# One stage for the rotation and the values' projection of a latent attention

## The chip, the cores and the metric

The kernel runs on one core of a Trainium2 chip. Its time is the device time of one execution in microseconds; the kernel before takes 3262.89 us, the median of three runs (3262.27 to 3264.33). The reader needs five of the core's engines: TensorE (PE, with its weight loads PEld), VectorE (DVE), ScalarE (ACT), GpSimd (POOL), and SyncE (SP), which issues DMA transfers here. Each works through its own list of instructions in order and waits on semaphores.

## The reference, cut to what matters

The program is two transformer blocks. The change lies in the second mixer of the first block, an attention over 256 context and 512 latent tokens whose keys and values come from a latent of 256 numbers per token:

```
def mla_q(q_a, q_norm, w_uq, rope):
    q = (rmsnorm(q_a, q_norm) @ w_uq).reshape(B, L, MLA_HEADS, MLA_NOPE + MLA_ROPE)
    q_n, q_r = jnp.split(q, [MLA_NOPE], axis=-1)
    return jnp.concatenate([q_n, apply_rope2d(q_r, *rope)], axis=-1)

def mla_kv(kv_a, k_r, kv_norm, w_ukv, rope):
    kv = (rmsnorm(kv_a, kv_norm) @ w_ukv).reshape(B, L, MLA_HEADS, MLA_NOPE + MLA_V)
    k_n, v = jnp.split(kv, [MLA_NOPE], axis=-1)
    if rope is not None:
        k_r = apply_rope2d(k_r, *rope)
    ...
```

Two things in it matter here. The rotated parts (64 numbers per head of the queries, 64 shared ones of the keys) go through `apply_rope2d`. The values v of all 8 heads are one product: 768 tokens by 256, times 256 by 1024.

## The kernel before, in words

The kernel is a sequence of stages. Each stage is one block: all engines start it together, after a barrier, and the next one starts when all have left it. Semaphores come from two sets that take turns; the GpSimd clears those of the stage before.

Every matrix product is made of three passes. An operand x is kept as two rounded parts, x.high (a copy on ACT in the type float32r) and x.low (on DVE, x minus x.high), and `three_passes` (L304 to L306) adds high*high, high*low and low*high into one bank of PSUM, the accumulator memory, which has 8 banks of 512 numbers per partition.

The attention's preparation is six stages in a row (function `mla`); the last three are those of the change:

1. `rotate_split` rotates five tiles of 128x512: four of queries, one of keys. Per tile: PE multiplies it with a permutation into one of banks 0 to 3 (L2336), DVE multiplies by the cosine (L2356), multiplies the bank by the sine (L2358) and adds both (L2359), ACT makes the high part (L2344), DVE the low part (L2352). A sixth piece, the context's keys, is only split (L2341 and L2352).
2. `project_tokens` for the first 512 columns of the values. SP loads 512 KB of weights (L1576), ACT and DVE split them in two steps (L1595, L1605), PE meanwhile runs eight products whose result nobody reads (`keep_running`, L290), then makes six sums, one for each 128 tokens, of six matmuls each. ACT copies a finished sum to v.high (L1599), DVE writes v.low (L1616), which frees the bank. Four banks are used in turn.
3. The same for the other 512 columns, over the same places for the weights.

After them the stage of the attention itself starts, whose first instruction on PE is a score's matmul (L304).

The queries and keys before rotation, the cosine, the sine and a scratch tile lie where v is written. The weights' place held the queries' latent, which nothing reads any more once these three stages begin. What is read of the latent of keys and values lies behind it.

Of the kernel before, what the change touches and what calls it, by code (L numbers as in the profile page):

```python
# [28 lines left out]
ALU = mybir.AluOpType  # L29
AX = mybir.AxisListType  # L30

P = 128
D = 1024
DT = D // P
CTX = 256
# [64 lines left out]
H_LOW_AT = DT * T  # L100
# [1463 lines left out]
def project_tokens(k, weights, dst, kt, x, token_tiles, width, col=None, at=None):  # L1564

    nc = k.nc
    k.stage()
    at = MEM - 3 * kt * width if at is None else at
    raw = k.plain(at, kt, width)
    w = Pair(k, at + kt * width, at + 2 * kt * width, kt, width)  # L1570
    landed, rounded, ready, product, cut, taken = (k.sem(s) for s in ("landed", "rounded", "ready", "product", "cut", "taken"))
    n_tiles = len(token_tiles)
    with k.block() as block:
        @block.sync
        def _(sp):
# [25 lines left out]
        @block.vector  # L1601
        def _(dve):
            for kk in range(kt):
                dve.wait_ge(rounded, kk + 1)
                nc.vector.tensor_tensor(w.low[:, kk, :], raw[:, kk, :], w.high_plain[:, kk, :],  # L1605
                                        ALU.subtract).then_inc(ready, 1)
            for j in range(n_tiles):
                if col is None:
                    dve.wait_ge(product, j + 1)
                    bank = k.bank(j % 4, width)  # L1610
                    parts = dst[:, j].shape
                    nc.vector.tensor_copy(dst[:, j], bank.rearrange("p (h n) -> p h n", n=parts[2]) if len(parts) == 3 else bank
                                          ).then_inc(taken, 1)
# [708 lines left out]
            in_turns(dve, turns, turn)  # L2322


def rotate_split(k, parts, cos, sin, scratch, plain=()):

    nc = k.nc
    k.stage()
    partner, summed, rounded = k.sem("partner"), k.sem("summed"), k.sem("rounded")
    with k.block() as block:  # L2330
        @block.tensor
        def _(pe):
            for n, (x, *out) in enumerate(parts):
                if n >= 4:
                    pe.wait_ge(summed, n - 3)
                nc.tensor.matmul(k.bank(n % 4), k.const("rot_gqa"), x, start=True, stop=True).then_inc(partner, 1)  # L2336

        @block.scalar
        def _(act):
            for x, high, high_plain, low in plain:  # L2340
                nc.scalar.copy(high, x).then_inc(rounded, 1)  # L2341
            for n, (x, high, high_plain, low) in enumerate(parts):
                act.wait_ge(summed, n + 1)
                nc.scalar.copy(high, x).then_inc(rounded, 1)  # L2344

        @block.vector
        def _(dve):
            chain = Chain(dve, k.sem("chain"))

            def cut(n, x, high, high_plain, low):  # L2350
                dve.wait_ge(rounded, n + 1)
                nc.vector.tensor_tensor(low, x, high_plain, ALU.subtract)  # L2352

            todo = list(plain) + list(parts)
            for n, (x, *out) in enumerate(parts):
                chain.link(nc.vector.tensor_tensor(scratch, x, cos, ALU.mult))  # L2356
                dve.wait_ge(partner, n + 1)
                chain.link(nc.vector.tensor_tensor(x, k.bank(n % 4), sin, ALU.mult))  # L2358
                nc.vector.tensor_tensor(x, x, scratch, ALU.add).then_inc(summed, 1)  # L2359
                dve.wait_ge(summed, n + 1)  # L2360
                for m in range(len(plain) if n == 0 else 0):
                    cut(m, *todo[m])
                if n:
                    cut(len(plain) + n - 1, *parts[n - 1])
            cut(len(todo) - 1, *parts[-1])


def load(k, pairs):
# [11 lines left out]
def mla(k, norm):  # L2380
    low = k.plain(MLA_V_AT, 6, T)
    qr_plain = k.plain(MLA_V_AT + 6 * T, 4, LAT)
    at = MLA_V_AT + 6 * T + 4 * LAT
    cos, sin, scratch = (k.words(at + j * LAT, at + (j + 1) * LAT) for j in range(3))
    qa = Pair(k, H_LOW_AT, H_LOW_AT + 3 * LAT, 3, LAT, CTX)
    kva = Pair(k, H_LOW_AT + 6 * LAT, H_LOW_AT + 6 * LAT + 2 * T, 2, T)
    kn = Pair(k, H_HIGH_AT, WORK_AT, 8, T)
    at = WORK_AT + 8 * T
    qn, at = Pair(k, at, at + 8 * LAT, 8, LAT, CTX), at + 16 * LAT
    qr, at = Pair(k, at, at + 4 * LAT, 4, LAT, CTX), at + 8 * LAT  # L2390
    kr = Pair(k, at, at + T, 1, T)
# [10 lines left out]
    rotate_split(k, [(qr_plain[:, n, :], qr.high[:, n, :], qr.high_plain[:, n, :], qr.low[:, n, :]) for n in range(4)]  # L2402
                 + [(low[:, 5, CTX:T], kr.high[:, 0, CTX:T], kr.high_plain[:, 0, CTX:T], kr.low[:, 0, CTX:T])],
                 cos, sin, scratch, [(low[:, 5, 0:CTX], kr.high[:, 0, 0:CTX], kr.high_plain[:, 0, 0:CTX], kr.low[:, 0, 0:CTX])])
# [1316 lines left out]
```

## Time and profile before

| | |
|---|---|
| median of three runs | 3262.89 us |
| the profiled execution's own time | 3258.2 us |
| its span, first to last instruction | 3256.1 us |
| TensorE busy | 2944.3 us, 90% |
| VectorE busy | 1692.2 us, 52% |
| ScalarE busy | 1211.8 us, 37% |
| mean granted TensorE clock | 0.948 of full |

The profile is of one execution. Times inside it are microseconds from the span's first instruction. The granted clock is the share of full speed that TensorE was given: 1.00 is 2.4 GHz, 0.50 is 1.2 GHz. In an interval's row "PEq" is PE's own instruction sequencer, so idle time that ended with it ended by a barrier or a branch and not by data. The three stages of the change run from 1493.6 to 1540.4 us.

### The profile page before, as it was taken

To read this page: it belongs to the slowest core of one execution; us is meant where nothing else is said; L and a number is where in the kernel's file an instruction comes from. 1 tells how busy PE (TensorE), PEld (TensorE's weight loads), DVE (VectorE), ACT (ScalarE), POOL (GpSimd) and SP (SyncE) were. 2 spreads that over 40 slices of the span, in tenths; PEclk is the share of its full clock that TensorE was granted. 3 is DMA by queue.
4 is the path that set the end of the run, shared out by engine and by line. 5 is a ranking of instruction groups with operands and counts; after the bars stand their busy time and mean duration, and the time that the engine had idled before them with its cause. 6 is when DMAs were issued, how large, how long until landed. Compare 5 with 4: busy or idle time off the path is not lost. (4 is left out here: it accounts for less than half of the span.)

```text
span 3256.1 us, 37947 instructions
## 1 busy us (share of the span) xinstructions
PE 2944.3 (90%) x14226; PEld 2338.0 (72%) x14226; DVE 1692.2 (52%) x2385; ACT 1211.8 (37%) x1621; POOL 167.1 (5%) x127
## 2 busy tenths in 40 slices
PE   7899988799999899897999999989878888899996
PEld 3674776687888888675777887867755567777775
DVE  5444323634767443434654343352366553788886
ACT  2320231424232232423433433244424323477774
POOL 0000001100011000000000000000000100122220
PEclk9899998899999999999999999999979799999998
DMA  8300110021345142110002221212200013699996
GB/s 356 127 27 13 52 52 2 27 90 52 123 147 175 59 149 97 52 36 26 1 27 89 92 103 64 95 60 84 77 8 1 1 52 125 252 366 355 361 339 243
DMA packets 76008, 362.78 MB, mean 111 GB/s; under 512 B 13170, under 2 KB 17043, under 8 KB 50292
## 3 DMA queue, kind: packets, MB, share of 16 engines
q1 hardware_dynamic: 62356, 327.66, 27.9%
q0 software_dynamic: 13536, 33.58, 3.0%
q8 instruction: 72, 1.18, 0.1%
q14 instruction: 44, 0.36, 0.0%
HBM read 360.67 MB, written 16.25 MB: 116 GB/s over the span
## 5 line engine op out<-in xcount | busy, mean ns | idle before, releaser
L304 PE MATMUL ps<-rounded,rounded 128*128 128x512 f32 (+3 forms) x3700 | 1377.0, 372 | 139.9 <-DVE rounded L2237 24.2
L305 PE MATMUL ps<-rounded,rounded 128*128 128x512 f32 (+3 forms) x3700 | 1337.6, 362 | 0.0
L306 PE MATMUL ps<-rounded,rounded 128*128 128x512 f32 (+3 forms) x3700 | 1336.0, 361 | 0.0
L304 PEld LDWEIGHTS ps<-rounded,rounded 128*128 128x128 f32 (+1 forms) x3700 | 706.6, 191 | 322.6 <-issue 113.8
L306 PEld LDWEIGHTS ps<-rounded,rounded 128*128 128x128 f32 (+1 forms) x3700 | 707.0, 191 | 107.2
L305 PEld LDWEIGHTS ps<-rounded,rounded 128*128 128x128 f32 (+1 forms) x3700 | 708.5, 191 | 94.8
L283 DVE TENSOR_TENSOR rounded<-work,rounded 128x1024 fp32r<-128x1024 f32 (+3 forms) x224 | 306.6, 1371 | 840.7 <-ACT rounded L279 840.4
L279 ACT CAST rounded<-work 128x1024 fp32r<-128x1024 f32 (+3 forms) x224 | 261.6, 1169 | 740.2 <-PE ps L306 617.2
L3472 DVE TENSOR_TENSOR rounded<-work,rounded 128x2048 fp32r<-128x2048 f32 x138 | 309.8, 2287 | 71.9 <-ACT rounded L3300 71.9
L3300 ACT CAST rounded<-work 128x2048 fp32r<-128x2048 f32 x138 | 259.5, 1915 | 78.0 <-PE ps L306 78.0
L290 PE MATMUL ps<-cst 128*128 128x256 f32 x530 | 143.7, 432 | 64.7 <-PEq L170 64.7
L290 PEld LDWEIGHTS ps<-cst 128*128 128x128 f32 x530 | 113.8, 220 | 90.3 <-issue 72.5
L279 ACT ACT_TABLE_LOAD x34 | 43.6, 1283 | 207.1 <-PE ps L306 198.4
L478 DVE SCALAR_TENSOR_TENSOR work<-work,silu_c 128x256 f32<-128x256 f32 x224 | 103.7, 484 | 13.1 <-DMA work<-in_ada_w 7.3
L2756 POOL TENSOR_TENSOR h<-work,row 128x2048 f32<-128x2048 f32 x2 | 9.2, 4637 | 1486.8 <-DVE row L2838 1486.8
L1017 DVE SCALAR_TENSOR_TENSOR work<-ps,vec,work 128x255 f32 (+4 forms) x116 | 72.5, 654 | 20.4 <-ACT work L987 14.4
L1095 ACT ACTIVATE work<-work 128x768 f32<-128x768 f32 (+1 forms) x44 | 32.6, 740 | 126.7 <-DVE work L1130 126.7
L2237 DVE TENSOR_TENSOR rounded<-ps,rounded 128x768 fp32r<-128x768 f32 (+1 forms) x64 | 52.3, 817 | 40.3 <-ACT rounded L2204 40.3
L1386 PE MATMUL ps<-work 128*128 128x512 f32 x160 | 71.1, 603 | 0.0
L3184 POOL DMA_INDIRECT y_rows<-h,whole x23 | 51.5, 2240 | 345.6 <-ACT h L3338 345.6
L787 PE MATMUL ps<-work,silu_c 128*2 128x512 f32 x128 | 58.5, 612 | 10.8 <-DMA work<-in_ada_w 10.8
L2231 DVE TENSOR_REDUCE row<-ps 128x1 f32<-128x768 f32 (+1 forms) x64 | 52.5, 820 | 18.0 <-PE ps L306 17.8
(487 smaller groups left out, 2486.8 us busy)
## 6 DMA issues: line engine op xcount, KB each, us to landing
work<-in_moe SPq DMA_DIRECT2D x138, 1024.0 KB, 7.4
work<-in_ffn_up SPq DMA_DIRECT2D x44, 1024.0 KB, 4.8
work<-in_ffn_down SPq DMA_DIRECT2D x66, 512.0 KB, 3.4
work<-in_ada_w SPq DMA_DIRECT2D x12, 2048.0 KB, 18.0
work<-in_ada_w POOLq DMA_DIRECT2D x48, 512.0 KB, 4.0
work<-in_w_out SPq DMA_DIRECT2D x16, 512.0 KB, 3.6
work<-in_w_gates SPq DMA_DIRECT2D x16, 512.0 KB, 3.5
work<-in_w_in_hy SPq DMA_DIRECT2D x12, 512.0 KB, 3.4
```

Source lines behind the costliest of these rows:

```text
L279: self.k.nc.scalar.copy(self.parts[s][0], self.raw[s]).then_inc(self.rounded[s], 1)
L283: self.k.nc.vector.tensor_tensor(self.parts[s][1], self.raw[s], self.high_plain[s], ALU.subtract).then_inc(self.ready[s], 1)
L290: k.nc.tensor.matmul(k.bank(bank, 2 * P), k.const("ident"), k.cst[:, 0:2 * P], start=True, stop=True)
L304: k.nc.tensor.matmul(out, sh, mh, start=start, stop=False)
L305: k.nc.tensor.matmul(out, sh, ml, start=False, stop=False)
L306: return k.nc.tensor.matmul(out, sl, mh, start=False, stop=stop)
L478: done = self.k.nc.vector.scalar_tensor_tensor(out=total, in0=tile, scalar=by, in1=total, op0=ALU.mult, op1=ALU.add)
L787: last = nc.tensor.matmul(k.bank(n % 2)[0:2, :], k.silu_c[:, kk, :], wide[n % 3][:, kk * 512:(kk + 1) * 512], start=kk == 0, stop=kk == DT ...
L1017: nc.vector.scalar_tensor_tensor(out=out, in0=k.pair(p)[:, lo + o:hi + o], scalar=k.col(conv_w, n + tiles * (o + taps // 2)), in1=out, op0 ...
L1386: last = nc.tensor.matmul(bank(group, part), tab[part][:, a, n * P:(n + 1) * P], src[:, a, :], start=a == 0, stop=a == count - 1)
L3300: nc.scalar.copy(ring.parts[:, c % ring.SPLIT, 0, :], ring.raw[c % ring.RAW]).then_inc(ring.rounded, 1)
L3472: V.tensor_tensor(ring.parts[:, s, 1, :], ring.raw[c % ring.RAW], ring.plain[:, s, 0, :], ALU.subtract).then_inc(ring.ready, 1)
```

## The change

`rotate_split` and the two calls of `project_tokens` become one stage, `rotate_and_values`. The rotation keeps banks 0 to 3, the twelve sums of the values use banks 4 to 7 in turn. Both transfers of weights are issued in this stage, the second one once the first weights are split. The splitting of the first weights stands on ACT after the second query tile, on DVE after the third turn. PE makes the first four sums as soon as it has the weights. Because v lies over the rotation's inputs, ACT waits for DVE's last low part (semaphore `left`) before it copies the first sum. The weights of the second half are split after all six sums of the first half are made. The eight idle products of both `project_tokens` are gone. `k.stage()` is called once in place of three times.

```
-def rotate_split(k, parts, cos, sin, scratch, plain=()):
+def rotate_and_values(k, parts, cos, sin, scratch, plain, names, v, x, at):
...
+    width, kt, n_tiles = 512, 2, 6
+    raw, w = k.plain(at, kt, width), Pair(k, at + kt * width, at + 2 * kt * width, kt, width)
...
+    tiles = [(half, j) for half in range(2) for j in range(n_tiles)]
+
+    def sums(m):
+        return k.bank(4 + m % 4, width)
...
+        @block.sync
+        def _(sp):
+            for half, name in enumerate(names):
+                if half:
+                    sp.wait_ge(w_ready, kt)
+                sp.dma_start(raw, k.dram[name].rearrange("p (k n) -> p k n", n=width)).then_inc(landed, 16)
+
         @block.tensor
...
+            for m, (half, j) in enumerate(tiles):
+                if m >= 4:
+                    pe.wait_ge(taken, m - 3)
+                for kk in range(kt):
+                    if j == 0:
+                        pe.wait_ge(w_ready, kt * half + kk + 1)
+                    last = three_passes(k, sums(m), x.tokens(kk, j * P, (j + 1) * P), w.tokens(kk, 0, width), kk == 0, kk == kt - 1)
+                last.then_inc(product, 1)
 
         @block.scalar
         def _(act):
+            def weights(half):
+                act.wait_ge(landed, 16 * half + 16)
+                for kk in range(kt):
+                    nc.scalar.copy(w.high[:, kk, :], raw[:, kk, :]).then_inc(w_high, 1)
...
+                if n == 1:
+                    weights(0)
+            act.wait_ge(left, 1)
+            for m, (half, j) in enumerate(tiles):
+                if m == n_tiles - 1:
+                    act.wait_ge(product, n_tiles)
+                    weights(1)
+                act.wait_ge(product, m + 1)
+                nc.scalar.copy(v.high[:, j, half * width:(half + 1) * width], sums(m)).then_inc(cut, 1)
 
         @block.vector
...
+                if n == 2:
+                    weights(0)
+            split_off(len(todo) - 1, *parts[-1]).then_inc(left, 1)
+            for m, (half, j) in enumerate(tiles):
+                if m == n_tiles - 1:
+                    weights(1)
+                dve.wait_ge(cut, m + 1)
+                columns = slice(half * width, (half + 1) * width)
+                nc.vector.tensor_tensor(v.low[:, j, columns], sums(m), v.high_plain[:, j, columns], ALU.subtract).then_inc(taken, 1)
...
-    for half in range(2):
-        project_tokens(k, f"mla_w_v{half}", v, 2, kva, range(6), 512, half * 512, H_LOW_AT)
```

The order of ACT's instructions before, from the start of the rotation to the end of the values. `rounded_34816` and `rounded_37632` are the high parts of queries and keys, `rounded_8192` of the weights, `rounded_44544` of v; L170, L1591 and L2338 are the ends and starts of stages.

```order
L2338 UNCONDITIONAL_BRANCH
L2341 CAST rounded_37632_6878<-work 128x256
L2344 CAST rounded_34816_6876<-work 128x512 x4
L2344 CAST rounded_37632_6878<-work 128x512
L170 UNCONDITIONAL_BRANCH
L1591 UNCONDITIONAL_BRANCH
L1595 CAST rounded_8192_8190<-h 128x512 x2
L1599 CAST rounded_44544_6880<-ps 128x512 x6
```

The same place on ACT now:

```order
L2371 CAST rounded_37632_6878<-work 128x256
L2374 CAST rounded_34816_6876<-work 128x512 x2
L2368 CAST rounded_8192_8090<-h 128x512 x2
L2374 CAST rounded_34816_6876<-work 128x512 x2
L2374 CAST rounded_37632_6878<-work 128x512
L2383 CAST rounded_44544_6880<-ps 128x512 x5
L2368 CAST rounded_8192_8090<-h 128x512 x2
L2383 CAST rounded_44544_6880<-ps 128x512 x7
```

The first weights' copies have moved ahead of the third query tile's, the second weights' ahead of the sixth sum's.

On DVE before, from the low part in the fourth turn of the rotation to the end of the first half of the values (`rounded_36864` and `rounded_38400` are low parts of queries and keys, `rounded_9216` of the weights, `rounded_50688` of v):

```order
L2352 TENSOR_TENSOR rounded_36864_6877<-work,rounded_34816_6876 128x512
L2356 TENSOR_TENSOR work<-work 128x512
L2358 TENSOR_TENSOR work<-ps,work 128x512
L2359 TENSOR_TENSOR work<-work 128x512
L2352 TENSOR_TENSOR rounded_36864_6877<-work,rounded_34816_6876 128x512
L2352 TENSOR_TENSOR rounded_38400_6879<-work,rounded_37632_6878 128x512
L170 UNCONDITIONAL_BRANCH
L1601 UNCONDITIONAL_BRANCH
L1605 TENSOR_TENSOR rounded_9216_8191<-h,rounded_8192_8190 128x512 x2
L1616 TENSOR_TENSOR rounded_50688_6881<-ps,rounded_44544_6880 128x512 x6
```

Now on DVE, from the low part in the third turn on. One row of two more subtractions of weights and one of the seven last low parts of v follow, then the stage ends:

```order
L2391 TENSOR_TENSOR rounded_36864_6877<-work,rounded_34816_6876 128x512
L2396 TENSOR_TENSOR rounded_9216_8091<-h,rounded_8192_8090 128x512 x2
L2400 TENSOR_TENSOR work<-work 128x512
L2402 TENSOR_TENSOR work<-ps,work 128x512
L2403 TENSOR_TENSOR work<-work 128x512
L2391 TENSOR_TENSOR rounded_36864_6877<-work,rounded_34816_6876 128x512
L2400 TENSOR_TENSOR work<-work 128x512
L2402 TENSOR_TENSOR work<-ps,work 128x512
L2403 TENSOR_TENSOR work<-work 128x512
L2391 TENSOR_TENSOR rounded_36864_6877<-work,rounded_34816_6876 128x512
L2391 TENSOR_TENSOR rounded_38400_6879<-work,rounded_37632_6878 128x512
L2417 TENSOR_TENSOR rounded_50688_6881<-ps,rounded_44544_6880 128x512 x5
```

The first weights' two subtractions stand between the third and fourth turn of the rotation, and nothing stands any more between the rotation's last low part and the first of v.

## Rows read from the trace of the kernel before

**Rows 1.** The head of the page.
```profile
span 3256.1 us, 37947 instructions
```

**Rows 2.** Busy time in four stretches: the three stages, most of the attention.
```profile
core 0: us, PE busy (x) PEld busy (x) DVE busy (x) ACT busy (x) POOL busy (x), PEclk, DMA share, GB/s
1493.60:1508.50 14.90, 4.53 (x10) 1.82 (x10) 13.86 (x21) 3.51 (x6) 0.00 (x0) 0.80 0.00 0
1508.70:1524.00 15.30, 13.79 (x52) 11.10 (x52) 5.45 (x8) 4.67 (x8) 0.00 (x0) 0.87 0.11 34
1524.10:1540.50 16.40, 12.16 (x52) 9.64 (x52) 5.45 (x8) 4.68 (x8) 0.00 (x0) 1.00 0.11 33
1550.00:1680.00 130.00, 129.27 (x756) 98.32 (x755) 86.47 (x155) 50.79 (x97) 0.00 (x0) 1.00 0.00 1
```

**Rows 3.** Waits from 1493 to 1541: us in total, times, longest.
```profile
ACT rounded L1595 <- DMA h<-in_mla_w_v: 10.5, 2, 5.9
```

**Rows 4.** Order of time, rotation: start, us, engine, line, what, xcount [idle before <-releaser].
```profile
1493.62 0.41 ACT L2341 CAST rounded<-work 128x256 fp32r<-128x256 f32 x1 [1.28 <-PEq L170]
1493.64 4.53 PE L2336 MATMUL ps<-work,cst 128*128 128x512 f32 x10 [2.15 <-PEq L170]
...
1498.81 0.62 ACT L2344 CAST rounded<-work 128x512 fp32r<-128x512 f32 x1 [1.89 <-DVE work L2359]
...
1501.59 0.69 DVE L2352 TENSOR_TENSOR rounded<-work,rounded 128x512 fp32r<-128x512 f32 x1
1502.20 0.68 DVE L2356 TENSOR_TENSOR work<-work 128x512 f32<-128x512 f32 x1
...
1504.37 0.69 DVE L2352 TENSOR_TENSOR rounded<-work,rounded 128x512 fp32r<-128x512 f32 x1
...
1507.15 1.34 DVE L2352 TENSOR_TENSOR rounded<-work,rounded 128x512 fp32r<-128x512 f32 x2
```

**Rows 5.** Order of time, first half of the values.
```profile
1508.75 0.34 SPq L1576 DMA_DIRECT2D h<-in_mla_w_v  x1
1508.80 5.58 PE L290 MATMUL ps<-cst 128*128 128x256 f32 x16 [10.63 <-PEq L170]
1512.34 1.14 ACT L1595 CAST rounded<-h 128x512 fp32r<-128x512 f32 x2 [4.57 <-DMA h<-in_mla_w_v]
...
1523.24 0.69 DVE L1616 TENSOR_TENSOR rounded<-ps,rounded 128x512 fp32r<-128x512 f32 x1 [0.66 <-ACT rounded L1599]
```

**Rows 6.** Order of time, second half of the values, and the attention's first matmul.
```profile
1524.20 0.34 SPq L1576 DMA_DIRECT2D h<-in_mla_w_v  x1
...
1529.15 1.14 ACT L1595 CAST rounded<-h 128x512 fp32r<-128x512 f32 x2 [5.94 <-DMA h<-in_mla_w_v]
...
1530.55 0.50 PE L304 MATMUL ps<-rounded,rounded 128*128 128x512 f32 x1 [2.60 <-DVE rounded L1605]
...
1532.24 0.59 ACT L1599 CAST rounded<-ps 128x512 fp32r<-128x512 f32 x1 [1.95 <-PE ps L306]
...
1533.61 0.59 ACT L1599 CAST rounded<-ps 128x512 fp32r<-128x512 f32 x1 [0.78 <-PE ps L306]
...
1539.67 0.69 DVE L1616 TENSOR_TENSOR rounded<-ps,rounded 128x512 fp32r<-128x512 f32 x1 [0.67 <-ACT rounded L1599]
1540.68 0.35 PE L304 MATMUL ps<-rounded,rounded 128*128 128x256 f32 x1 [1.67 <-PEq L170]
```

**Rows 7.** Busy time and granted clock in four stretches.
```profile
485.30:488.60 3.30, 3.05 (x7) 2.47 (x8) 3.30 (x7) 3.12 (x6) 0.00 (x0) 0.50 0.00 0
1502.40:1505.80 3.40, 0.00 (x0) 0.00 (x0) 3.26 (x6) 0.62 (x1) 0.00 (x0) 0.50 0.00 0
1690.20:1693.50 3.30, 2.81 (x13) 2.81 (x14) 0.77 (x2) 0.00 (x0) 0.00 (x0) 0.50 0.00 0
2557.20:2598.00 40.80, 36.66 (x100) 21.02 (x101) 18.63 (x16) 11.82 (x40) 8.01 (x2) 0.50 0.00 1
```

**Rows 8.** Order of time: PE after idle time, elsewhere in the program.
```profile
485.55 0.79 PE L304 MATMUL ps<-rounded,rounded 128*128 128x512 f32 x1 [5.83 <-DVE rounded L1605]
...
486.57 0.63 PE L306 MATMUL ps<-rounded,rounded 128*128 128x512 f32 x1
487.00 0.63 PE L304 MATMUL ps<-rounded,rounded 128*128 128x512 f32 x1
...
1690.69 0.58 PE L304 MATMUL ps<-rounded,rounded 128*128 128x256 f32 x1 [1.88 <-DVE rounded L2237]
```

More of the change, by code:

```diff
@@ L2322, in _ @@
             in_turns(dve, turns, turn)
-def rotate_split(k, parts, cos, sin, scratch, plain=()):
+def rotate_and_values(k, parts, cos, sin, scratch, plain, names, v, x, at):
     nc = k.nc
     k.stage()
-    partner, summed, rounded = k.sem("partner"), k.sem("summed"), k.sem("rounded")
-    with k.block() as block:
+    width, kt, n_tiles = 512, 2, 6
+    raw, w = k.plain(at, kt, width), Pair(k, at + kt * width, at + 2 * kt * width, kt, width)
+    partner, summed, rounded, left = (k.sem(s) for s in ("partner", "summed", "rounded", "left"))
+    landed, w_high, w_ready, product, cut, taken = (k.sem(s) for s in ("landed", "w_high", "w_ready", "product", "cut", "taken"))
+    tiles = [(half, j) for half in range(2) for j in range(n_tiles)]
+    def sums(m):
+        return k.bank(4 + m % 4, width)
+    with k.block() as block:
+        @block.sync
[4 more added lines that the diff above has]
+                sp.dma_start(raw, k.dram[name].rearrange("p (k n) -> p k n", n=width)).then_inc(landed, 16)
@@ L2331, in _ @@
         @block.tensor
         def _(pe):
-            for n, (x, *out) in enumerate(parts):
+            for n, (y, *out) in enumerate(parts):
                 if n >= 4:
                     pe.wait_ge(summed, n - 3)
-                nc.tensor.matmul(k.bank(n % 4), k.const("rot_gqa"), x, start=True, stop=True).then_inc(partner, 1)
+                nc.tensor.matmul(k.bank(n % 4), k.const("rot_gqa"), y, start=True, stop=True).then_inc(partner, 1)
+            for m, (half, j) in enumerate(tiles):
[6 more added lines that the diff above has]
+                last.then_inc(product, 1)
@@ L2338, in _ @@
         @block.scalar
         def _(act):
-            for x, high, high_plain, low in plain:
-                nc.scalar.copy(high, x).then_inc(rounded, 1)
-            for n, (x, high, high_plain, low) in enumerate(parts):
-                act.wait_ge(summed, n + 1)
-                nc.scalar.copy(high, x).then_inc(rounded, 1)
+            def weights(half):
+                act.wait_ge(landed, 16 * half + 16)
+                for kk in range(kt):
+                    nc.scalar.copy(w.high[:, kk, :], raw[:, kk, :]).then_inc(w_high, 1)
@@ new lines, in _ @@
+            for y, high, high_plain, low in plain:
+                nc.scalar.copy(high, y).then_inc(rounded, 1)
+            for n, (y, high, high_plain, low) in enumerate(parts):
+                act.wait_ge(summed, n + 1)
+                nc.scalar.copy(high, y).then_inc(rounded, 1)
+                if n == 1:
[7 more added lines that the diff above has]
+                nc.scalar.copy(v.high[:, j, half * width:(half + 1) * width], sums(m)).then_inc(cut, 1)
@@ L2348, in _, with split_off, weights @@
             chain = Chain(dve, k.sem("chain"))
-            def cut(n, x, high, high_plain, low):
+            def split_off(n, y, high, high_plain, low):
                 dve.wait_ge(rounded, n + 1)
-                nc.vector.tensor_tensor(low, x, high_plain, ALU.subtract)
+                return nc.vector.tensor_tensor(low, y, high_plain, ALU.subtract)
+            def weights(half):
+                for kk in range(kt):
+                    dve.wait_ge(w_high, kt * half + kk + 1)
+                    nc.vector.tensor_tensor(w.low[:, kk, :], raw[:, kk, :], w.high_plain[:, kk, :], ALU.subtract).then_inc(w_ready, 1)
             todo = list(plain) + list(parts)
-            for n, (x, *out) in enumerate(parts):
-                chain.link(nc.vector.tensor_tensor(scratch, x, cos, ALU.mult))
+            for n, (y, *out) in enumerate(parts):
+                chain.link(nc.vector.tensor_tensor(scratch, y, cos, ALU.mult))
                 dve.wait_ge(partner, n + 1)
-                chain.link(nc.vector.tensor_tensor(x, k.bank(n % 4), sin, ALU.mult))
-                nc.vector.tensor_tensor(x, x, scratch, ALU.add).then_inc(summed, 1)
+                chain.link(nc.vector.tensor_tensor(y, k.bank(n % 4), sin, ALU.mult))
+                nc.vector.tensor_tensor(y, y, scratch, ALU.add).then_inc(summed, 1)
                 dve.wait_ge(summed, n + 1)
                 for m in range(len(plain) if n == 0 else 0):
-                    cut(m, *todo[m])
+                    split_off(m, *todo[m])
                 if n:
-                    cut(len(plain) + n - 1, *parts[n - 1])
-            cut(len(todo) - 1, *parts[-1])
+                    split_off(len(plain) + n - 1, *parts[n - 1])
+                if n == 2:
[7 more added lines that the diff above has]
+                nc.vector.tensor_tensor(v.low[:, j, columns], sums(m), v.high_plain[:, j, columns], ALU.subtract).then_inc(taken, 1)
 def load(k, pairs):
@@ L2401, in mla @@
     project_split(k, "mla_w_kn", kn, SEGS, 2, kva)
-    rotate_split(k, [(qr_plain[:, n, :], qr.high[:, n, :], qr.high_plain[:, n, :], qr.low[:, n, :]) for n in range(4)]
+    rotate_and_values(k, [(qr_plain[:, n, :], qr.high[:, n, :], qr.high_plain[:, n, :], qr.low[:, n, :]) for n in range(4)]
                  + [(low[:, 5, CTX:T], kr.high[:, 0, CTX:T], kr.high_plain[:, 0, CTX:T], kr.low[:, 0, CTX:T])],
-                 cos, sin, scratch, [(low[:, 5, 0:CTX], kr.high[:, 0, 0:CTX], kr.high_plain[:, 0, 0:CTX], kr.low[:, 0, 0:CTX])])
-    for half in range(2):
-        project_tokens(k, f"mla_w_v{half}", v, 2, kva, range(6), 512, half * 512, H_LOW_AT)
+                 cos, sin, scratch, [(low[:, 5, 0:CTX], kr.high[:, 0, 0:CTX], kr.high_plain[:, 0, 0:CTX], kr.low[:, 0, 0:CTX])],
+                      ("mla_w_v0", "mla_w_v1"), v, kva, H_LOW_AT)
     def rope_half(h):
```

## The prediction

> **What bounds the kernel now.** I read the head of the page first, for the span of 3256.1 us [rows 1], then the busy time by stretches, then who waits for whom, then the order of time. In the stretches the reader is to see that the three stages differ from the attention behind them. The attention has TensorE busy for 129.27 of 130 us; there only PE's work counts. The rotation has PE busy for 4.53 of 14.90 us and DVE for 13.86: it is bound by DVE. The two halves of the values hold the same 52 matmul records each, 16 of them idle products, and DVE is busy for 5.45 us in either [rows 2]. So PE is idle for most of the first stage, and DVE for most of the other two. In the waits the reader sees a second loss: ACT waits 10.5 us for the two transfers of weights [rows 3], since each is issued only when its own stage opens.
>
> In the order of time the rotation starts at 1493.6 and PE's ten records (five matmuls) are over at 1493.64 + 4.53 = 1498.17, while DVE ends at 1507.15 + 1.34 = 1508.49 [rows 4]. The first half then takes to 1523.24 + 0.69 = 1523.93 [rows 5], the second to 1540.36, and the attention's first matmul starts at 1540.68 [rows 6]. All that the change touches lies between 1493.6 and 1540.68. From the end of the rotation to the end of v are 1540.36 - 1508.49 = 31.87 us, and this is what I rebuild.
>
> **The first weights, under the rotation.** SP issues the transfer at about 1493.6. From issue to ACT's first copy the two transfers of before took 1512.34 - 1508.75 = 3.59 us [rows 5] and 1529.15 - 1524.20 = 4.95 us [rows 6]. ACT comes to the weights after its second query tile, at 1498.81 + 0.62 = 1499.43 [rows 4], 5.8 us after the issue: it finds them. Its two copies take 1.14 us [rows 6], to 1500.57. ACT's next tile is summed no sooner than 1501.59, where DVE goes on in step with it [rows 4], so ACT loses nothing. DVE reaches its two subtractions at 1502.20 and they stand in its list ahead of the fourth turn: a real cost, as DVE bounds the rotation. Two such subtractions are 1.34 us [rows 4]. If the transfer came later than about 7.5 us after its issue, each further microsecond would be one on DVE; I cost it at nothing, with the longer of the two transfers 2.5 us short of that.
>
> So the rotation ends at 1508.49 + 1.34 = 1509.83. **PE** has its first weights after one subtraction, at 1502.20 + 0.67, about 1502.9, and starts on four sums, 24 matmuls. In the steady pace of before a sum takes 1533.61 - 1532.24 = 1.37 us, 0.228 a matmul [rows 6], so the four would take 5.5 us.
>
> **The clock.** PE has then been idle from 1498.17 to 1502.9, 4.7 us. Nothing keeps it busy, since the idle products are gone. In the same stretch before, the granted clock had fallen to 0.50 by 1502.40 [rows 7], and a values' projection elsewhere, which also started after idle time (5.83 us), began at 0.50, with matmuls 487.00 - 486.57 = 0.43 us apart in place of 0.228 [rows 7, 8]. So I take the fall as certain. That one lasted from its first matmul at 485.55 to about 488.6, 3.1 us. At 0.43 all 24 matmuls take 10.3 us (to 1513.2); with 3 us at the low clock they take about 7 (to 1510). The bounds of this item at the point where the sums are needed: ACT copies the first at 1509.83 and, DVE behind it taking 0.69 a sum, the fourth is wanted from about 1511.7. With a low clock of up to 6 us the fourth is made by 1511.5 and the cost is zero; with one that lasts throughout, 1.5 us on this part alone. I take zero, the nearest row being the 3.1 us one. The Trainium skill, page "TensorE: Matmul & The Clock Gate", section "Why this matters for your kernels", warns against letting PE idle between bursts of matmuls, since the clock then falls back to half rate. By this rule alone, dropping the idle products speaks against the change. Taken to its end, with no recovery before the attention, it gives the time of the second rival below (3259.6); the sum here gives 3248.0. The row agrees that the clock falls; what the rule does not weigh is that these four sums wait for the rotation anyway.
>
> **From the rotation's end.** ACT was held by `left`; queued behind that wait are all of v's copies, and behind these DVE's low parts and, for its fifth sum on, PE. First copy 0.59, its low part 0.69 [rows 6], and 0.1 for the hand-overs between engines (an estimate: DVE idles 0.67 before a low part, 0.08 more than ACT's copy takes [rows 6]): the first bank is free at 1509.83 + 1.38 = 1511.21. PE makes sums five and six, and ACT sees the sixth 1.69 + 1.37 = 3.06 us after PE's start (1530.55 to 1532.24, and one more pace) [rows 6]: 1514.27. The second weights, issued at about 1503.5 when the first are split, have long landed (4.95 us at most in the rows of before), 5.8 us earlier. Splitting them stands exposed, since it overwrites what PE was reading: from ACT's first copy to PE's first matmul 1530.55 - 1529.15 = 1.40 us [rows 6]: 1515.67. DVE has by then worked off five sums and does the sixth while PE runs. From there the stage is the old second half: 1540.36 - 1530.55 = 9.81 us [rows 6], to 1525.48. The stage ends with the same 0.32 us of barrier (1540.36 to 1540.68).
>
> **Sum:** 1.34 + 1.38 + 3.06 + 1.40 + 9.81 = 16.99 us in place of 31.87: 14.9 us less. It is made up of two openings of a stage with their transfers (3.85 and 5.22 us from the last DVE instruction to ACT's first copy), one splitting of weights, and four sums, against 1.34 us more on DVE and the first drain. The stage uses 11 semaphores in place of 4 + 6 + 6; GpSimd clears them beside the rest and shows no busy time here [rows 2]. The profiled execution takes 3258.2 us, 2.1 more than its span, and would take 3243.3. It lies 4.7 us under the median, 3262.89; the same difference off the median gives **3248.0 us**, 0.46% less.
>
> **Rivals.**
>
> A second fall of the clock. Between sums four and five PE idles up to 1 us, between six and seven 1.4 us. For a fall: after a matmul-poor stretch with an idle time of 1.88 us the clock was at 0.50 [rows 7, 8]. Against: the second half of before idles 1.67 and 2.60 us and keeps 1.00 throughout [rows 2, 6]. A low stretch of about 3.3 us, as that one, loses near half of itself: 1.6 us, 3249.6.
>
> The clock stays low to the end of v. For: 40.80 us at 0.50 with PE busy for 36.66 of them exist in this trace [rows 7], and no idle products lift it here. Against: those are largely smaller matmuls (100 in 36.66 us, 0.37 each, against 0.63 for a 128x512 one at that clock [rows 8]), and the 128x512 ones of the values at 485 us came back after 3.1. Price: four sums end at 1513.2, the next two 12 x 0.43 = 5.2 and a last matmul's tail of 0.2 later, at 1518.6 (4.3 late), the second half takes 36 x (0.43 - 0.228) = 7.3 more: 14.9 - 11.6 = 3.3 us gained, 3259.6, which counts as no change.
>
> The other side: the clock stays low into the attention. The stage then ends at 1537.1 and each further microsecond at 0.50 loses 0.47 of PE's time, which bounds there. The gain is used up when the clock has not come back by 1544, 41 us after PE's restart, so the longest low stretch of the trace would just decide it. If it lasted 60 us, the loss would be 12.1 - 3.3 = 8.8 us: 3271.7, slower. Against it speaks that the attention of before holds 1.00 at 99% busy [rows 2].
>
> The change doesn't deliver its overlap: the first weights land late, or DVE and ACT slow down with PE beside them. A landing 5 us after the point of 7.5 us costs 5: 3253. Against: DVE's 128x512 instructions take 0.69 us beside an idle PE and beside a busy one [rows 4, 6].
>
> **How the numbers follow.** The forecast gets 0.78, the second fall 0.10 (3249.6), late weights or a slower overlap 0.05 (3253), the clock low to the end of v 0.04 (3259.6), low into the attention 0.03 (3271.7). A measurement of this kernel tells a change from none at about 0.2%, 6.5 us, so from 3256.4 down it is faster: 0.78 + 0.10 + 0.05 = 0.93; same 0.04; slower 0.03. For the range: the forecast's own terms vary with the transfer and the hand-overs by 1 us, with the clock under the rotation by 1.5 us, and the runs by 2 us between each other. 3244.5 to 3252.5 holds the first two cases.
>
> **What would show it.** In the profile after: PE's first L304 of the stage about 9.3 us after its start and at 0.50; four sums made before ACT's first copy of v, or within 2 us of it; no wait of ACT for the first transfer; one wait of PE for the second weights of about 1.4 us; clock 1.00 through the last six sums; stage from start to attention's first matmul 32.2 us in place of 47.1. I am wrong if that length is over 35 us, or if it is right and the whole did not move with it.

## The result, and the profile after

| | median | lowest to highest | runs |
|---|---|---|---|
| before | 3262.89 us | 3250.51 to 3279.56 | 7 |
| after | 3242.97 us | 3234.40 to 3259.34 | 7 |

The ratio is 0.9934, 95% interval 0.9908 to 0.9960: the change makes the kernel faster, by 21 us (13 to 30) as the ratio has it. Predicted were 14.9 us and 3248.0; the measured median lies 1.5 us under the low end of the range, 3244.5. Two more comparisons of the same kernel gave 0.9958 and 0.9957 (below).

The head of the page after, which answers to [rows 1]; the span is 23.5 us shorter:

```profile
span 3232.6 us, 37859 instructions
```

Busy time by stretches: to the rotation's end, to the start of the second half's sums, to the attention's first matmul; then the low clock, and the attention. The columns are those of [rows 2].

```profile
1491.90:1508.10 16.20, 11.37 (x28) 7.22 (x29) 15.07 (x23) 4.59 (x9) 0.00 (x0) 0.79 0.20 65
1508.10:1514.00 5.90, 4.39 (x20) 3.24 (x19) 4.00 (x7) 4.18 (x8) 0.00 (x0) 1.00 0.00 0
1514.00:1524.10 10.10, 8.43 (x36) 6.69 (x37) 5.22 (x8) 3.72 (x8) 0.00 (x0) 1.00 0.00 0
1500.40:1507.00 6.60, 5.74 (x14) 4.48 (x15) 6.39 (x11) 1.07 (x3) 0.00 (x0) 0.50 0.25 79
1524.10:1678.90 154.80, 149.70 (x864) 114.09 (x864) 97.57 (x176) 59.89 (x113) 0.00 (x0) 0.99 0.00 1
```

PE is busy 11.37 us during the rotation where it was busy 4.53; DVE is nearly full there in both. The low clock lies wholly under the rotation: it began 1.0 us before PE's first sum and ended at 1507.1.

The order of time in the stage after, to be read against [rows 4 to 6]:

```profile
1491.91 10.27 SPq L2346 DMA_DIRECT2D h<-in_mla_w_v  x2
1491.96 4.53 PE L2353 MATMUL ps<-work,cst 128*128 128x512 f32 x10 [2.15 <-PEq L170]
...
1497.66 1.14 ACT L2368 CAST rounded<-h 128x512 fp32r<-128x512 f32 x2
...
1500.52 1.28 DVE L2396 TENSOR_TENSOR rounded<-h,rounded 128x512 fp32r<-128x512 f32 x2
1501.26 0.79 PE L304 MATMUL ps<-rounded,rounded 128*128 128x512 f32 x1 [4.77 <-DVE rounded L2396]
...
1508.06 1.57 ACT L2383 CAST rounded<-ps 128x512 fp32r<-128x512 f32 x3 [0.76 <-DVE rounded L2391]
...
1508.68 2.49 DVE L2417 TENSOR_TENSOR rounded<-ps,rounded 128x512 fp32r<-128x512 f32 x4 [0.65 <-ACT rounded L2383]
...
1512.53 1.14 ACT L2368 CAST rounded<-h 128x512 fp32r<-128x512 f32 x2 [0.77 <-PE ps L306]
...
1514.02 0.47 PE L304 MATMUL ps<-rounded,rounded 128*128 128x512 f32 x1 [1.53 <-DVE rounded L2396]
...
1523.10 0.69 DVE L2417 TENSOR_TENSOR rounded<-ps,rounded 128x512 fp32r<-128x512 f32 x1 [0.66 <-ACT rounded L2383]
...
1524.11 0.35 PE L304 MATMUL ps<-rounded,rounded 128*128 128x256 f32 x1 [1.67 <-PEq L170]
```

The row 1497.66 has no idle time behind it: ACT did not wait for the weights. ACT's copies of v begin right after the rotation's last low part, and PE's only wait between 1501.26 and the last sum is the 1.53 us for the second weights. From 1491.96 to 1524.11 are 32.15 us; before it was 1540.68 - 1493.64 = 47.04. The stage gives **14.89 us**; 14.9 was predicted.

So 23.5 - 14.9 = 8.6 us of the two spans' difference lie elsewhere, in code that the change leaves alone. 1.7 us are won ahead of the stage (it starts at 1491.96 in place of 1493.64). The largest other piece is one stage of the second block's scan, which takes 93.6 us before and 89.6 after. First before, then after:

```profile
2548.40:2642.00 93.60, 75.50 (x368) 48.25 (x368) 50.51 (x78) 34.27 (x99) 9.24 (x2) 0.75 0.00 0
```

```profile
2528.90:2618.50 89.60, 70.92 (x368) 45.44 (x368) 50.43 (x78) 34.30 (x99) 9.24 (x2) 0.80 0.00 1
```

The same 368 matmuls, DVE's and ACT's work the same to 0.1 us; what differs is the granted clock, 0.75 against 0.80, and PE's time with it. Whether this belongs to the change was the first question for the runs.

### The profile page after: what moved, and what is told of

Same layout as the page of the kernel before. It is cut to its first block and busy times, and to the rows that moved or that the text cites. A ratio compares the mean times of both kernels' runs of the same rounds, so it can differ in the third digit from the quotient of the medians.

```text
span 3232.6 us, 37859 instructions
## 1 busy us (share of the span) xinstructions
PE 2925.2 (90%) x14194; PEld 2321.4 (72%) x14194; DVE 1691.8 (52%) x2385; ACT 1212.0 (37%) x1621; POOL 168.0 (5%) x127
## 5 line engine op out<-in xcount | busy, mean ns | idle before, releaser
L290 PE MATMUL ps<-cst 128*128 128x256 f32 x498 | 134.6, 431 | 53.5 <-PEq L170 53.5
L290 PEld LDWEIGHTS ps<-cst 128*128 128x128 f32 x498 | 107.2, 221 | 77.1 <-issue 60.4
L2237 DVE TENSOR_TENSOR rounded<-ps,rounded 128x768 fp32r<-128x768 f32 (+1 forms) x64 | 52.3, 817 | 40.4 <-ACT rounded L2204 40.4
L2231 DVE TENSOR_REDUCE row<-ps 128x1 f32<-128x768 f32 (+1 forms) x64 | 52.4, 819 | 17.9 <-PE ps L306 17.7
```

Of the source, the lines that this page charges most:

```text
L290: k.nc.tensor.matmul(k.bank(bank, 2 * P), k.const("ident"), k.cst[:, 0:2 * P], start=True, stop=True)
```

## The experiments

Two theories stood against each other. **A:** the gain is the stage's 14.9 us, and the rest is where the clock happened to be low in an execution. **B:** later stages are shorter because of the change. All comparisons are with runs of the kernel before on the same chip. "Stage" is from the rotation's first matmul to the attention's first, "attention" from there to the first matmul of the stage behind it, both in one profiled execution.

| run | stage, profiled | attention, profiled | ratio | 95% interval |
|---|---|---|---|---|
| before (first profile) | 47.0 | 154.9 | | |
| r_before | 50.0 | 164.5 | 1.0005 | 0.9984 to 1.0025 |
| after (first profile) | 32.2 | 155.1 | 0.9934 | 0.9908 to 0.9960 |
| r_after | 32.1 | 163.2 | 0.9958 | 0.9944 to 0.9972 |
| r_after2 | 32.1 | 164.6 | 0.9957 | 0.9937 to 0.9977 |
| e_late_sums | 38.6 | 164.2 | 0.9986 | 0.9958 to 1.0013 |
| e_prefetch | 45.4 | 154.9 | 1.0010 | 0.9992 to 1.0028 |
| e_prefetch_bare | 42.0 | 155.4 | 0.9986 | 0.9965 to 1.0008 |
| e_warm | 33.4 | 154.8 | 0.9968 | 0.9949 to 0.9987 |
| e_bridge | 33.8 | 154.4 | 0.9943 | 0.9921 to 0.9965 |
| e_cold_entry | 35.1 | 165.5 | 0.9991 | 0.9972 to 1.0011 |
| e_eight | 26.9 | 164.6 | 0.9956 | 0.9930 to 0.9981 |
| e_eight_bridge | 27.9 | 154.9 | 0.9905 | 0.9886 to 0.9924 |
| r_eight_bridge | 26.9 | 154.9 | 0.9902 | 0.9868 to 0.9936 |

### The same kernels again

The edit is none.

> The changed kernel once more, unaltered. Theory A (the gain is the stage's 14.9 us, what the first comparison showed beyond it is where TensorE's clock happened to be low): the stage takes 32.2 us again, from its first instruction to the attention's first matmul, the ratio to the kernel before comes out at 1 - 14.9/3262.9 = 0.9954 and its interval holds that; outside the stage the stages that were shorter than before in the first comparison (after the attention, 6.8 us together) do not all come out shorter. Theory B (the change shortens later stages as well): ratio 0.9934 again, the same later stages shorter.

> The kernel before, unaltered, as a comparison of the kernel with itself. Theory A (the times scatter because TensorE's clock falls at other places in each execution): ratio 1.000 within its interval, the three stages of the change 47.0 us again, and the span off the first profile's 3256.1 by several us, with the difference in stages whose low-clock time differs. Theory B (the stages outside the change take the same time in each execution of one kernel): every stage within 0.3 us of the first profile's.

> The changed kernel a third time, beside the others. Stage 32.1 to 33.8 us, ratio 0.9954 within its interval; the mean over the three comparisons then decides between 14.9 us and the first comparison's 21.

Stages of 32.13 and 32.11 us, ratios 0.9958 and 0.9957: 13.7 and 14.0 us of 3259. The three ratios weighted by their intervals give 0.9954, 15.0 us, give or take 3.4. The scan's stage took 93.6 us in r_after, 89.6 in r_after2 and 97.5 in r_before, and 89.6 in e_prefetch_bare, a variant of the kernel before: the first pair's 4.1 us were not the change's. Theory A holds, B fell.

One expectation of r_before missed: its three stages took 50.0 us and not 47.0. The clock was low in two more places there. The idle products of the first half ran at the low clock for longer (6.69 us for 5.58), and after 2.79 us without work PE's sums of the second half started low, at 0.50 from 1529.1 to 1532.5; in the first profile of before, 2.60 us without work had left them at 1.00. So the gain of the stage is 14.9 us from one pair of profiles and 17.9 from another.

The changed kernel repeats better. In r_after and r_after2 the low stretch under the rotation lasted 3.4 to 3.5 us in place of 6.8, so PE had its four sums earlier, and it waited 0.80 and 0.85 us for a free bank ahead of the fifth. The stage is the same to 0.04 us in all three.

What I had not expected is the attention, whose instructions are the same in all these kernels. Three stretches of it, of r_before, r_after and r_after2:

```profile
1540.70:1705.00 164.30, 160.19 (x864) 121.41 (x864) 97.90 (x176) 59.78 (x113) 0.00 (x0) 0.92 0.00 1
```

```profile
1523.50:1686.40 162.90, 158.93 (x864) 119.97 (x864) 97.94 (x176) 59.72 (x113) 0.00 (x0) 0.93 0.00 1
```

```profile
1526.70:1691.00 164.30, 160.23 (x864) 121.44 (x864) 97.97 (x176) 59.75 (x113) 0.00 (x0) 0.91 0.00 1
```

Again 864 matmuls and the same work on DVE and ACT, yet 8 to 10 us more than in the first profile of before or after (149.7 us of PE in 154.8 us there). In r_after the clock fell about 1.1 us after the attention's first matmul. The order of time, then the stretch that follows:

```profile
1523.49 0.35 PE L304 MATMUL ps<-rounded,rounded 128*128 128x256 f32 x1 [1.67 <-PEq L170]
...
1524.35 0.27 PE L306 MATMUL ps<-rounded,rounded 64*128 64x256 f32 x1
1524.55 0.74 PE L304 MATMUL ps<-rounded,rounded 128*128 128x512 f32 x1
```

```profile
1524.60:1548.50 23.90, 23.90 (x71) 16.57 (x71) 9.82 (x18) 5.47 (x11) 0.00 (x0) 0.50 0.00 0
```

PE's records fill all 23.90 us, and the clock still stays at 0.50. Half of the attention's score matmuls use 64 rows (the row at 1524.35 is one), but so they do in the executions that keep 1.00. It happens to the kernel before as well: r_before shows such a stretch from 1542.8 to 1566.7. All five profiles with a long attention and 1.67 us of idle time ahead of it (r_before, r_after, r_after2, e_late_sums, e_eight) have one of 23.9 us, which begins 1.0 to 2.1 us behind the attention's first matmul; the five short ones have none.

### The fall of the clock at the attention's start

One kernel makes sure that PE is idle for long ahead of the attention, one fills the idle time.

```
e_cold_entry, on DVE behind the last low part:
+            for _ in range(4):
+                chain.link(nc.vector.tensor_tensor(raw[:, 0, :], raw[:, 1, :], raw[:, 1, :], ALU.add))
e_bridge, on PE behind the last sum:
+            keep_running(k, 3, 0)
```

> The changed kernel with four useless additions on DVE (128x512, 0.72 us each, 2.9 us) behind v's last low part, so that PE idles 4.6 us ahead of the attention in every execution. If a fall of the clock at the attention's start costs about 8 us (as in the repeated runs of the changed kernel and of the kernel before: 163.2 and 164.5 us in place of 154.9), the attention takes 162 to 165 us here in the profile too, and the median lies 2.9 plus most of 8.5 us above the changed kernel's: ratio to the kernel before 0.998 to 0.999. Rival (the clock comes back after some 3 to 4 us, as elsewhere): attention 156 to 157 us, ratio 0.9965 to 0.997.

> The changed kernel with three idle products (six records, about 1.4 us) behind the last sum, while ACT and DVE drain it. In the repeated run of the changed kernel the clock fell 1.1 us after the attention's first matmul and stayed low for 23.9 us, and the attention took 163.2 us in place of 154.9. If PE's idle time of 1.67 us ahead of the attention lets that happen, the attention now holds 1.00 at its start, the stage stays at 32.2 us, and the median lies 2 to 4 us under the changed kernel's. Rival (the fall comes from the attention's own start, whatever stands ahead): the same falls in some executions and the same median.

With PE idle for 4.65 us the attention starts at the low clock and takes 165.5 us; the ratio is 0.9991, against 0.9957 of r_after2 beside it: 11 us, with some 9 us of uncertainty on the difference; forecast were 2.9 and most of 8.5. The first row is its first matmul, 0.55 us long in place of 0.35; the second its attention:

```profile
1531.15 0.55 PE L304 MATMUL ps<-rounded,rounded 128*128 128x256 f32 x1 [4.65 <-PEq L170]
```

```profile
1531.10:1696.40 165.30, 161.22 (x864) 122.27 (x864) 97.96 (x176) 59.74 (x113) 0.00 (x0) 0.90 0.00 1
```

With three idle products PE waits 0.37 us ahead of the attention, and the attention took 154.4 us. In the three profiles with these products (e_bridge, e_eight_bridge, r_eight_bridge) it never was long; in the ten with the plain 1.67 us it was long in five. Three short ones in a row would come out once in eight times even if the products did nothing, so this points to their worth and does not prove it. The ratio of e_bridge, 0.9943, lies 1.5 thousandths under r_after's, and the intervals overlap: by these times its worth is not shown either. What e_cold_entry shows is the other end, in one profile: after 4.65 us without work the attention ran low. The stage took 33.8 us and not 32.2, for the reason in the next experiment.

### A warm clock ahead of the sums

```
e_warm, on PE between the rotation's matmuls and the sums:
+            keep_running(k, 9)
```

> The changed kernel with nine idle products of 256 columns (18 records, about 4.2 us) between the rotation's matmuls and the values' first sum, in the time in which PE waits. My account: the granted clock stays at 1.00, the four sums end about 2 us earlier, and nothing else moves: stage 32.2 us again. Rival (the fall of the clock costs the stage something): stage 30.5 to 31.5 us. A second rival: the fillers run past the weights' arrival and delay the sums, stage unchanged still.

None of the three came out: the stage grew by 1.2 us, to 33.4. The clock stayed at 1.00 and the four sums ended early, as expected, but then PE had nothing to do until the first bank came free, and the clock fell after that wait. Of e_warm, the fifth sum's first matmul and its fourth:

```profile
1513.29 0.50 PE L304 MATMUL ps<-rounded,rounded 128*128 128x512 f32 x1 [2.40 <-DVE rounded L2418]
...
1514.79 0.63 PE L304 MATMUL ps<-rounded,rounded 128*128 128x512 f32 x1
```

The duration of 0.63 is that of the low clock [rows 8]. e_bridge shows the same without fillers ahead of the sums. There the rotation's matmuls had run at the low clock (6.23 us for 4.53), PE was idle for only 3.18 us after them, and the first four sums ran at 1.00. PE then waited 2.41 us, and the fifth and sixth sum ran slow:

```profile
1510.94 0.50 PE L304 MATMUL ps<-rounded,rounded 128*128 128x512 f32 x1 [2.41 <-DVE rounded L2418]
1511.27 0.59 PE L305 MATMUL ps<-rounded,rounded 128*128 128x512 f32 x1
1511.66 0.63 PE L306 MATMUL ps<-rounded,rounded 128*128 128x512 f32 x1
```

So the fall under the rotation costs nothing, as predicted, and is even the better case: slow sums leave a short wait behind them or none. The prediction's rival of a second fall is real. Its price was about right (1.2 and 1.7 us for 1.6), but it needs a longer wait than the "up to 1 us" it was derived from: waits of 0.80 and 0.85 us (r_after, r_after2) brought no fall.

### What the parts are worth

```
e_late_sums, on PE ahead of the sums:
+            pe.wait_ge(left, 1)
e_prefetch and e_prefetch_bare, on the kernel before:
+        @block.sync
+        def _(sp):
+            sp.dma_start(k.plain(H_LOW_AT, 2, 512), k.dram[first[0]].rearrange("p (k n) -> p k n", n=512)).then_inc(first[1], 16)
...
+            if next_ is not None:
+                sp.wait_ge(ready, kt)
+                sp.dma_start(raw, k.dram[next_[0]].rearrange("p (k n) -> p k n", n=width)).then_inc(next_[1], 16)
e_prefetch_bare alone:
-            keep_running(k)
+            if here is None:
+                keep_running(k)
```

> The changed kernel with one wait more: TensorE starts the first sum only when the rotation's last low part is written (the wait for `left` ahead of all sums). The weights still come under the rotation. My account: PE starts at 16.2 us into the stage, at the low clock for 3 to 6 us (1.4 to 2.8 us lost), the six sums end 8.5 us later plus that, then 1.4 + 9.8 + 0.3: stage 38.3 us (37.7 to 39.1), so 8.7 of the 14.9 us stay. Rival (the sums under the rotation are worth only what is not drained later, little): stage under 35 us.

> The kernel before with its three stages; only the two transfers of weights are issued one stage earlier, and the idle products at the start of either half, which covered the transfers, are left out. My account: the first half starts its sums 1.7 us into its stage at the low clock and ends about 1.8 us earlier than before, the second half 4.9 us earlier: the three stages take 40.4 us (39.6 to 41.2) in place of 47.1, under half of the change's gain. Rival (nearly all of the gain is the hidden transfers): 34 us or less.

> The kernel before in three stages with either transfer of weights one stage earlier, and this time really without the idle products at the start of either half (the run named e_prefetch had kept them, and PE worked through them while the weights lay ready). My account: 40.4 us (39.6 to 41.2) for the three stages in place of 47.0, so 5.9 to 7.4 of the 14.9 us, the rest being the sums under the rotation. Rival: 34 us or less.

Holding the sums back gave 38.6 us against 38.3 forecast: 6.5 us of the gain are gone, 8.4 stay. About 1 us of the 6.5 has another cause: in this profile the rotation's first product was made at the low clock, DVE waited 1.47 us for it in place of 0.52, and PE started 17.1 us into the stage and not 16.2. Without that, the sums under the rotation are worth about 5.5 us and the rest about 9.4, and the closeness to 38.3 is in part luck. e_prefetch missed (45.4 for 40.4), but it was not the kernel its expectation describes: it still had the idle products, and PE worked through them with the weights lying ready. Without them the three stages took 42.0 us, 0.8 over the top of the forecast, at a mean clock of 0.80 where I had counted one low stretch: it fell at the rotation's start, under the rotation and again after 3.03 us of idle time in the second half. Earlier transfers alone give 5.0 us by this profile (5.8 without the 0.8 that DVE waited longer for the rotation's first product), the whole change about three times as much; the rival (34 us or less) is out. The ratios of these three can't be told from 1.

### A version that beats both

```
e_eight; e_eight_bridge and r_eight_bridge have the last two lines besides
-        return k.bank(4 + m % 4, width)
+        return k.bank((4, 5, 6, 7, 1, 2, 3, 0)[m % 8], width)
...
-                if m >= 4:
-                    pe.wait_ge(taken, m - 3)
+                if m >= 8:
+                    pe.wait_ge(taken, m - 7)
+                elif m >= 4:
+                    pe.wait_ge(summed, m - 2)
... ACT: weights(0) after n == 0, weights(1) ahead of the wait for left
... DVE: weights(0) after n == 1, weights(1) behind the rotation
+            pe.wait_ge(taken, 6)
+            keep_running(k, 3, 1)
```

> A version meant to beat both: the changed kernel with the first weights split after the first copy of ACT and the second turn of DVE, the sums in all eight banks (4 to 7, then 1, 2, 3, 0), the second weights split right behind the rotation, ahead of v's first low part, and three idle products behind the last sum. PE's first sum at 6.5 us into the stage (9.3 in the changed kernel), six sums made before the rotation ends; second half of the sums from 16.9; DVE the bound then, with twelve low parts of 0.72 from 17.5 on: 26.5 + 0.3 = 26.9 us (26.4 to 27.8) in place of 32.2. Whole time about 5.3 us under the changed kernel. Rival (the low clock or a bank's wait eats it): 30 us or more.

> The version with eight banks, without the three idle products behind the last sum. Stage 26.9 us again (27.9 with a low clock at its start). Where the idle products matter by keeping the attention from starting low, the attention is long (about 163 us) in some executions and the median is 2 to 3 us above that with them; where they don't, the same median.

> The version with eight banks and the idle products once more. From the stages alone 14.9 + 5.3 = 20.2 us and 1 to 3 us from the attention's start: ratio 0.9929 to 0.9938. The first comparison gave 0.9905, which I hold for chance by the scatter of the clock; if it is 0.9905 again, something beyond the stage is shorter as well.

The stage came out at 26.9 us in two profiles, as forecast, and at 27.9 in the third, e_eight_bridge. There the clock was low for the rotation's very first matmul, and DVE waited 1.47 us for its product in place of 0.52:

```profile
1499.88 0.69 DVE L2405 TENSOR_TENSOR work<-ps,work 128x512 f32<-128x512 f32 x1 [1.47 <-PE ps L2353]
```

In e_eight the clock fell only 1.0 us later, behind the first product, and the stage lost nothing. Of r_eight_bridge: PE's first sum, its wait for the second weights, eight copies of v in a row on ACT and nine low parts on DVE, and the three idle products:

```profile
1497.18 0.50 PE L304 MATMUL ps<-rounded,rounded 128*128 128x512 f32 x1 [2.00 <-DVE rounded L2399]
...
1506.94 4.14 ACT L2386 CAST rounded<-ps 128x512 fp32r<-128x512 f32 x8
1507.47 0.47 PE L304 MATMUL ps<-rounded,rounded 128*128 128x512 f32 x1 [1.84 <-DVE rounded L2399]
1507.84 5.46 DVE L2419 TENSOR_TENSOR rounded<-ps,rounded 128x512 fp32r<-128x512 f32 x9
...
1515.74 1.46 PE L290 MATMUL ps<-cst 128*128 128x256 f32 x6
```

PE's first sum stands 6.5 us into the stage and six are made before v may be written. With the idle products the ratios are 0.9905 and 0.9902 (medians 3235.99 and 3227.79), without them 0.9956 (3245.20). The difference is larger than the 2 to 3 us expected. The intervals of e_eight and r_eight_bridge just overlap (0.9930 to 0.9936), but five of the six times of r_eight_bridge (3224 to 3229) lie under all twelve of e_eight on the same chip. The twelve fall into two groups, six from 3229 to 3241 and six from 3250 to 3262. It is tempting to read them as short and long attentions, but one profile speaks against that: e_eight_bridge's execution of 3254.1 us had a short attention. Lengths of the same stages in the three profiles, in us ("last" is the program's last stage):

| profile | span | stage | attention | the scan's stage | last |
|---|---|---|---|---|---|
| e_eight | 3252.2 | 26.9 | 164.6 | 97.5 | 510.0 |
| e_eight_bridge | 3252.3 | 27.9 | 154.9 | 97.6 | 510.8 |
| r_eight_bridge | 3226.3 | 26.9 | 154.9 | 89.6 | 505.5 |

The last two are one and the same kernel, 26.0 us apart with the same attention: 8.0 us of that lie in the scan, 5.3 in the last stage, 1.0 in the stage of the change, the rest in others. So the attention's start is one draw of 8 to 10 us among several. That the idle products take it away fits all profiles; that it makes up the 17 us between the medians of e_eight and r_eight_bridge is not shown, and it cannot be the whole, as a short attention saves 10 us at most.

Against the kernel before, the stages give 20.1 us, and the two comparisons 31 (25 to 37) and 32 (21 to 43). If before has a long attention in half of its executions, as the plain kernels' profiles have, removing it is worth some 5 us more on average. That estimate, 25 us, lies at the low end of both intervals; what is beyond it was not traced.

## Why the prediction was right or wrong

**The stage: right in size and, but for one tie, in its path.** Rebased to the stage's start (the prediction's times less 1.68), measured against predicted: first sum 1501.26 for 1501.2; ACT's first copy of v 1508.06 for 1508.15; second weights' split 1512.53 for 1512.59; PE on them 1514.02 for 1513.99; attention 1524.11 for 1524.12. The 1.34 us on DVE, the drain, the 3.06, the 1.40 and the 9.81 us all stood in the rows of before, and code of the same shape took the same time. The tie is at the fifth sum. The prediction has PE wait there for a bank, free at 1509.53 rebased. In this profile PE came from the fourth sum just then, at 1509.58, and did not wait; in r_after and r_after2 it did, 0.80 and 0.85 us. The path was the one predicted in these two, and either way the stage took 32.1 us.

**The clock under the rotation: right.** It fell and was low until 1507.1, 5.8 us after PE's restart, inside the "up to 6 us" that cost nothing, though with next to nothing to spare. In the two repetitions it was low for 3.4 to 3.5 us, as in the row at 485 us that the prediction went by.

**The total: the interval holds the forecast, the range missed the median by 1.5 us.** The step that failed is in "How the numbers follow": "the runs by 2 us between each other". That came from three runs, 3262.27 to 3264.33. Seven runs of before spread over 29 us, seven of after over 25. With such a scatter the difference of two medians of seven is off by some 8 us (the half width of the interval, 0.0026 of 3263), and a range of 8 us in all, about a gain forecast to 1 us, was too narrow by a factor of two. The forecast was of the gain; the measured time is of the gain and a draw. Repeated, the gain was 13.7 and 14.0 us. No term of the 16.99 us sum was found wrong; the one that failed is this scatter, put at 2 us and measured at 25 to 29, and its source shows in the profiles as stages outside the change at another mean clock (the attention 154.9 or 163.2 to 164.6 us, the scan's stage 89.6, 93.6 or 97.5).

**The rival on the slower side: right place, wrong argument.** I gave it 0.03 and dismissed it with "the attention of before holds 1.00 at 99% busy". One profile can't show that. In five of ten profiles with the plain entry it didn't hold. But it is not the fall under the rotation that lasts, as the rival had it: the clock recovers, and may fall anew at the attention's start, for 23.9 us, at a price of 8 to 10 us, in the kernel before too. Since it strikes both, it widens the scatter and hardly moves the difference.

**The second fall inside the stage** happened in two of the variants (e_warm, e_bridge) and in none of the three profiles of the changed kernel. The argument against it, that the second half of before "idles 1.67 and 2.60 us and keeps 1.00 throughout", rested on one execution too: in r_before the same place idled 2.79 us and started low.

**The rule on idle PE** from the Trainium skill, page "TensorE: Matmul & The Clock Gate", section "Why this matters for your kernels", which warns against idle gaps between bursts of matmuls: the trace agrees, the clock fell in 4.77 us without work, and for the four sums that cost nothing. At the attention's entry a far shorter gap, 1.67 us, came before a fall in half of the profiles, and the low clock outlasted a stretch in which PE had no idle time at all.

## What to carry to other kernels

Small stages in a row that are bound by different engines can be merged, and the result can be computed from the rows of before, if what may overlap is read from what overwrites what (here one wait, `left`, and one place for two sets of weights). It came out to 0.1 us for this kernel and for e_eight; where the clock fell at a place that the sum had at full speed, the variants missed by 1.0 to 1.7 us (e_warm, e_bridge, e_prefetch_bare, e_eight_bridge) and before itself by 3.0 (r_before). Before a range is given around such a sum, the scatter of the whole must be known from more than three runs: where PE's clock falls and returns by chance, stages that nobody touched move by 4 to 10 us. And the products that keep PE busy are best tried where the next stage is sensitive to the clock (here in front of the attention, where the evidence is good but not complete); where PE's work waits for something else anyway they gained nothing and cost 1.2 us (e_warm).

## What the runs showed of the hardware that was not expected

- The attention, once at 0.50, stayed there for 23.9 us in five of five profiles, with PE's records covering all of it; half of its score matmuls use 64 rows, in the executions at 1.00 as well. Values' matmuls of 128x512 at the low clock came back 3.1 us [rows 7, 8] and 5.8 us (after) behind their first matmul.
- How long PE idled at the entry went with what followed: idle for 0.37 us ahead of the attention gave 154.4 to 154.9 us in three of three, 1.67 us gave 154.8 to 155.4 or 163.2 to 164.6, half and half, 4.65 us gave 165.5 (one profile).
- PE at full clock ahead of a wait made that wait longer (2.40 and 2.41 us in e_warm and e_bridge), and the clock fell after it: a filler in one place moved the fall to a worse one. A wait of 2.60 us brought no fall in one profile of before, 2.79 us did in another.
